# Unread matmuls in four layer norms, and three MLP units side by side behind two of them

## What is computed

```python
def _layer_norm(x, g, b):
    xf = x.astype(jnp.float32)
    mu = jnp.mean(xf, -1, keepdims=True)
    var = jnp.mean(jnp.square(xf - mu), -1, keepdims=True)
    return ((xf - mu) * lax.rsqrt(var + LN_EPS) * g + b).astype(x.dtype)

def _sq_relu_mlp(x, w1, w2):
    return jnp.square(jax.nn.relu(x @ w1)) @ w2

    for layer in range(DEPTH):
        ...
        x = _layer_norm(DEEPNORM_ALPHA * x + h, ln1_g[layer], ln1_b[layer])
        x = _layer_norm(DEEPNORM_ALPHA * x + _sq_relu_mlp(x, mlp_w1[layer], mlp_w2[layer]),
                        ln2_g[layer], ln2_b[layer])
```

## Time and profile before

| | us |
|---|---|
| median of 3 runs | 3241.9 (3241.63 to 3243.15) |
| profiled execution | 3248.51 |
| its span | 3246.7 |
| TensorE busy | 3161.2 (97%) |
| VectorE busy | 1778.5 (55%) |
| ScalarE busy | 1182.9 (36%) |
| GpSimd busy | 190.0 (6%) |
| mean granted TensorE clock, share of full | 0.982 |

### The profile page before, as it was taken

How to read it: one execution, slowest core, us unless ns; L and a number is a source line. 1 busy time by engine, 2 the same in 40 slices (tenths; PEclk the granted TensorE clock), 3 DMA queues, 4 the chain that set the end, 5 groups by cost and what they waited for, 6 DMA issues and landing times.

```text
span 3246.7 us, 42028 instructions
## 1 busy us (share of the span) xinstructions
PE 3161.2 (97%) x17280; PEld 2505.5 (77%) x17280; DVE 1778.5 (55%) x2750; ACT 1182.9 (36%) x1849; POOL 190.0 (6%) x149
## 2 busy tenths in 40 slices
PE   9999899999999889999899999999999999999999
PEld 6788778888777678887677687788877758778887
DVE  3753463343777754344577545654647754566463
ACT  4543243232444434232353423432335342343232
POOL 1221020001000020000100000000010000010000
PEclk9999899999999989999899999999999999999999
DMA  4210022222222112222212122223232212222322
GB/s 170 78 51 20 2 80 102 91 91 92 73 72 72 65 52 89 93 91 91 100 65 78 52 94 93 97 77 111 81 114 77 67 51 91 91 91 86 102 94 75
DMA packets 41563, 264.88 MB, mean 82 GB/s; under 512 B 4600, under 2 KB 4984, under 8 KB 13980
## 3 DMA queue, kind: packets, MB, share of 16 engines
q1 hardware_dynamic: 41364, 262.18, 23.7%
q10 hardware_dynamic: 8, 0.01, 0.0%
HBM read 260.07 MB, written 3.42 MB: 81 GB/s over the span
## 4 chain that ended last, share of the span: by engine, by line
PE 79%; DVE 6%; ACT 3%; issue 1%; DVEq 0%; ACTq 0%; POOL 0%; POOLq 0%
PE psum L340 23%; PE psum L342 23%; PE psum L341 23%; PE psum L1029 2%; ACT tiles L1067 1%; DVE tiles L1091 1%; PE psum L2017 1%; PE psum L2016 1%; PE psum L2018 1%; DVE w_lo L321 1%; PE psum L1928 1%; PE psum L1936 1%; PE psum L1038 1%; PE psum L690 1%; PE psum L1020 1%
## 5 line engine op out<-in xcount | busy, mean ns | idle before, releaser
L340 PE MATMUL psum<-hi,w_hi 128*128 128x512 f32 x3608 | 1447.0, 401 | 18.2 <-DVE w_lo L321 9.1
L341 PE MATMUL psum<-lo,w_hi 128*128 128x512 f32 x3608 | 1427.3, 396 | 0.0
L342 PE MATMUL psum<-hi,w_lo 128*128 128x512 f32 x3608 | 1427.2, 396 | 0.0
L313 ACT ACTIVATE w_hi<-ring 128x1024 fp32r<-128x1024 f32 (+1 forms) x495 | 505.1, 1021 | 889.0 <-PE psum L342 825.6
L340 PEld LDWEIGHTS psum<-hi,w_hi 128*128 128x128 f32 x3608 | 678.5, 188 | 189.2 <-DVE lo L590 10.2
L321 DVE TENSOR_TENSOR w_lo<-ring,w_hi 128x1024 fp32r<-128x1024 f32 (+1 forms) x495 | 592.9, 1199 | 421.4 <-ACT w_hi L313 421.3
L341 PEld LDWEIGHTS psum<-lo,w_hi 128*128 128x128 f32 x3608 | 678.5, 188 | 168.5 <-issue 7.0
L342 PEld LDWEIGHTS psum<-hi,w_lo 128*128 128x128 f32 x3608 | 677.7, 188 | 165.9
L772 DVE SCALAR_TENSOR_TENSOR xT<-xT,psum 128x512 f32<-128x512 f32 x96 | 65.9, 687 | 224.8 <-PE psum L342 224.8
L1067 ACT ACTIVATE tiles<-tiles,small 128x256 f32<-128x256 f32 (+3 forms) x176 | 95.0, 541 | 159.6 <-DVE small L1091 159.1
L1676 DVE TENSOR_TENSOR tiles<-tiles 128x512 f32<-128x512 f32 x64 | 44.3, 692 | 173.4 <-ACT tiles L1668 173.4
(11 more groups left out here) (262 smaller groups left out, 2749.6 us busy)
## 6 DMA issues: line engine op xcount, KB each, us to landing
ring<-in_weights SPq DMA_DIRECT2D x211, 1024.0 KB, 4.8
ring<-in_weights SPq DMA_DIRECT2D x28, 704.0 KB, 4.0
ring<-in_weights SPq DMA_DIRECT2D x4, 896.0 KB, 4.5
ring<-in_weights SPq DMA_DIRECT2D x3, 832.0 KB, 4.3
xT<-in_x SPq DMA_DIRECT2D x8, 256.0 KB, 5.4
tiles<-bias_repeated SPq DMA_DIRECT2D x8, 256.0 KB, 7.1
out<-xT SPq DMA_DIRECT2D x8, 256.0 KB, 2.8
held<-in_const SPq DMA_DIRECT2D x1, 1344.0 KB, 7.6
```

The source lines that it names most:

```text
L313: act.activation(self.w_hi[:, n % AHEAD, 0:UNITS[n] * P], self.raw(n), ACT.Copy).then_inc(self.hi_ready, 1)
L340: pe.matmul(out, hi, rhs.hi(first + at), start=(at == 0), stop=False)
L341: pe.matmul(out, hi, rhs.lo(first + at), start=False, stop=False)
L342: last = pe.matmul(out, lo, rhs.hi(first + at), start=False, stop=(at == end))
```

## The change

It has two parts.

First, matmuls whose result nobody reads. `idle` issues `count` matmuls in plain f32 into a bank: the 128x128 identity as weights, the 512 columns of `mask` (an attention mask in SBUF, mostly zeros) streamed past them. In `Moments.sums` one stands behind the first group of sums and one behind the last; in `layer_norm` three stand behind the second spread. All go to bank 4. So that bank 4 is free, the wait for the sixth residual tile (`added`, 6) moves up in front of the first of them. That makes five at each of the four norms, twenty in all.

Second, `three_products` takes the place of `two_products` in `squared_relu` (behind the first and the third norm). Two units run along with the arriving tiles as before, and a third follows `LAG` = 3 tiles behind. `two_products` stays behind the second and the fourth norm.

```diff
+LAG = 3
...
+    def idle(self, pe, count, bank):
+        for n in range(count):
+            pe.matmul(self.bank(bank), self.c("ident"), self.mask[:, :], start=True, stop=True)
+
+    def three_products(self, pe, outs, n, rhs, rhs_ready):
+        pe.wait_ge(self.lo_ready, n + 2)
+        for i in range(DT + LAG):
+            if i < DT:
+                pe.wait_ge(rhs_ready, i + 1)
+            if i == LAG:
+                pe.wait_ge(self.lo_ready, n + 3)
+            for u, at, out in ((n, i, outs[0]), (n + 1, i, outs[1]), (n + 2, i - LAG, outs[2])):
+                if 0 <= at < DT:
+                    w = slice(at * P, (at + 1) * P)
+                    hi, lo = self.w_hi[:, u % AHEAD, w], self.w_lo[:, u % AHEAD, w]
+                    pe.matmul(out, hi, rhs.hi(at), start=(at == 0), stop=False)
+                    pe.matmul(out, hi, rhs.lo(at), start=False, stop=False)
+                    last = pe.matmul(out, lo, rhs.hi(at), start=False, stop=(at == DT - 1))
+                    if at == DT - 1:
+                        last.then_inc(self.unit_used, 1)
...
         token_sums(pe, sq_out, self.acc, column, last=False)
+        pe.wait_ge(self.added, 6)
+        self.k.idle(pe, 1, 4)
         pe.wait_ge(self.diff_summed, DT - 2 - SHIFT)
-        pe.wait_ge(self.added, 6)
         token_sums(pe, diff_out, self.diff, column, last=False)
         pe.wait_ge(self.shifted, DT)
         token_sums(pe, diff_out, self.k.x(DT - 1), column, first=False).then_inc(self.diff_done, 1)
         pe.wait_ge(self.squared, DT)
         token_sums(pe, sq_out, self.sq[(DT - 1) % 2], column, first=False).then_inc(self.sq_done, 1)
+        self.k.idle(pe, 1, 4)
...
             spread_tokens(k, pe, k.bank(7), rstd, 1).then_inc(spread_done, 1)
+            k.idle(pe, 3, 4)
...
-            k.two_products(pe, [k.bank(0), k.bank(1)], first, rhs, rhs_ready)
-        elif t == 1 and rhs_ready is not None:
+            k.three_products(pe, [k.bank(0), k.bank(1), k.bank(2)], first, rhs, rhs_ready)
+        elif t in (1, 2) and rhs_ready is not None:
             return
```

## The result

| | before | after |
|---|---|---|
| median of 18 runs, us | 3242.7 (3240.9 to 3248.6) | 3250.2 (3243.5 to 3254.3) |
| ratio, 95% interval | 1 | 1.0018 (1.0012 to 1.0025) |
| span of the profiled execution, us | 3246.7 | 3248.5 |
| its mean granted TensorE clock | 0.982 | 0.987 |

The changed kernel is slower by 0.18%, 5.8 us by the ratio (3.9 to 8.1), 7.5 by the medians. The measured time lies in the predicted range. The forecast was +6.1 us (3248.0). All of these lie at the edge of what counts as no change (6.5 us). The profiled execution of the change took 3250.3 us, which is at the median of its runs; that of the kernel before took 3248.5, among the longest of its runs.

The account below looks back on a forecast made before the run. TensorE, busy 97% of the span near full clock, was taken as the bound. Clock falls at about three of four norms, 2.0 us each, gave +6.1 us over the median 3241.9: 3248.0 us, range 3240.5 to 3255.

Parts of the forecast that it names:

- Prices: TensorE at the norms: one unread matmul 0.86 us, a group of sums 0.89 us at full clock; 1.72 and 1.67 at half.
- Parts one and two: Unread matmuls among and behind the sums, before the first spread: each delays VectorE's centring 0.86 us, 1.72 per norm at equal clock.
- Part three: Three unread matmuls behind the last spread: full clock for first products gains at most 1.04, 1.4, 0.7 us; fourth norm none.
- Part four: Three units side by side behind the first and third norm: 0.1 us gained at each over two units, 0.2 in all.
- How often the clock falls, and what a fall costs: At the norms: the clock falls at about three of four, some later than now, so 2.0 instead of 2.35 us each.
- the +0.3 that was worked out for a full clock: Second norm, clock staying full: centring 1.7 us later, products gain 1.4, net +0.3 us.
- A: Rival: the clock holds at all four norms, delay and gain cancel, 0 us, 3241.9 us; chance 0.20.
- B: Rival: unread matmuls don't count as work for the clock, three behind the spread run at half; +16 us, 3258; chance 0.07.
- C: Rival: holes in the sums hide the first two unread matmuls and the clock holds; -6.5 to -7 us, 3235; chance 0.05.
- D: Rival: side-by-side units starve the next split, 1 to 2 us at first and third norm; inside the range, no separate chance.

Follow-up runs that it names:

- sums_alone: Kernel before plus only the two unread matmuls among and behind the sums at each norm, two units side by side: 1.0021 against the kernel before, +6.8 us.
- doubled_sums: The change with two unread matmuls instead of one in each place among and behind the sums: 1.0030 against the kernel before, +9.7 us.
- tail_alone: Kernel before plus only the three unread matmuls behind the second spread, two units side by side: 0.9991 against the kernel before, -2.9 us.
- three_alone: The change without any unread matmul, three units side by side behind the first and third norm: 0.9997 against the kernel before.
- unread_alone: The change with two units side by side as before, all five unread matmuls per norm kept: 1.0021 against the kernel before, +6.8 us.
- second_alone: Kernel before plus only the one unread matmul behind the sums at each norm: 1.0006 against the kernel before, +1.9 us.
- tail_three: The change without the two unread matmuls among and behind the sums; three behind the spread and three units stay: 0.9989 against the kernel before, -3.6 us.
- five_behind: The change with all five unread matmuls of each norm behind the second spread, three units side by side: 0.9988 against the kernel before, -3.9 us.
- first_alone: Kernel before plus only the one unread matmul among the sums at each norm: 1.0003 against the kernel before, +1.0 us.
- first_tail: The change without the unread matmul behind the sums; one among them, three behind the spread, three units: 0.9994 against the kernel before, -1.9 us.

## Why the prediction was right, and where its steps were off

**Prices.** The unread matmul was put at 0.86 us from rows of the same shape; in the changed profile one group of sums and one of them take 1.75 us (435.25 to 437.00), which is 0.89 + 0.86, and the six records behind the spread last 2.74 us, five steps of 0.43 and one record of 0.59. Right.

**Parts one and two, the chain.** +1.72 us per norm at equal clock. Measured at the second norm 6.38 against 4.66 us: right to 0.01. That a delay of the norms is passed on is seen in the profiles of sums_alone and doubled_sums, 4.5 and 9.3 us when the second block's row is reached. That all of it is passed on is not shown: at the fourth norm of the change 1.1 of the 1.7 us are.

**Part three, the clock's gain.** Forecast at most 1.0, 1.4 and 0.7 us at the first three norms; the 48 products took 1.0, 1.4 and 0.7 us less in tail_alone. In all -2.9 us by the ratio (0 to -5.8), against the 1.04 + 1.4 + 0.7 = 3.1 of the bounds. Right.

**Part four.** +-0.2 us, measured -1.0 (-3.6 to +1.9): not told from nothing, as said.

**How often the clock falls, and what a fall costs.** I took three of four norms, at 2.0 us each. In the profile it falls at three of four, later than before at the first and third norm (4.2 us after the dense work) and, at the fourth, only at 1586.4, behind the norm's spreads. Centring was 1.7, 1.7, 1.4 and 1.7 us late, where I had allowed 3.4 and 2.7 to 3.5 for a fall at the old moment. The number of falls was right; the price of one was not. Between the same VectorE instructions in both profiles (430.2 to 500.7, 803.5 to 860.1, 1190.1 to 1260.1 and 1561.8 to 1612.1 us before), the change takes 0.6, 0.3, 0.6 and 1.1 us longer: 2.6 us for the four norms, where 6.1 were forecast. The second norm is the +0.3 that was worked out for a full clock; the first and third cost 0.6 each with a fall, not 2.0. The step that was off is therefore this term, three falls at 2.0 us. One profile cannot give its mean (over the same four stretches three_alone, whose norms are those of before, is 2.1 us shorter than before), but the ratio of the runs (+5.8) does not confirm 2.0 either, because more than the norms goes into it, as the part on the spans shows. That the total came out near +6.1 is in part luck.

**Rivals.** A (the clock holds, 0 us): the number is excluded by the interval, and the clock fell at three norms of the profile. But the 2.6 us of its four norms lie between A's 0 and the forecast. B (unread matmuls don't count for the clock): excluded by the second norm, which held full clock for 11.3 us of sums, spreads and unread matmuls, and by the first products at full clock. C (holes hide them): excluded by the queue without holes and by sums_alone. D: no idle time of TensorE ahead of the next unit.

The Trainium skill, page "TensorE: Matmul & The Clock Gate", section "Part 4: PE-mode transpose", says that a matmul in transpose mode does not count as busy for the clock in the same way. Nothing here contradicts it; but a plain matmul with the identity as weights and a mostly zero stream does count: the second norm held the full clock for 11.3 us over the sums, the spreads and all five of them.

**The spans of the two profiles, and a term that the sum lacks.** The prediction gave 3252.8 us for the span of the changed kernel, if profiled: 6.1 more than before. It was 3248.5, 1.8 more. All of the 1.8 is there when the second block's row is reached (2.6 lost at the norms, 1.2 won back between 1100 and 1190 us, where the clock was low for 20.5 us instead of 23.9, and some 0.4 elsewhere); behind that both executions take the same time. So where is the rest of the +5.8 of the runs? The row consists mostly of matmuls on half the array (L1928, L1936). Where it begins and the first product behind it, in the profile of before:

```profile
2608.28 1.12 PE L1928 MATMUL psum<-tiles 64*128 64x512 f32 x2
...
2642.31 0.50 PE L340 MATMUL psum<-hi,w_hi 128*128 128x512 f32 x1
```

The same two in the changed kernel, then in second_alone:

```profile
2610.11 1.12 PE L1957 MATMUL psum<-tiles 64*128 64x512 f32 x2
...
2644.14 0.50 PE L341 MATMUL psum<-hi,w_hi 128*128 128x512 f32 x1
```

```profile
2608.28 1.12 PE L1955 MATMUL psum<-tiles 64*128 64x512 f32 x2
...
2637.52 0.50 PE L341 MATMUL psum<-hi,w_hi 128*128 128x512 f32 x1
```

34.0 us, 34.0 us and 29.2 us for the same work. The difference is the clock. Before, then second_alone (columns as in the earlier trace rows):

```profile
2615.60:2625.00 9.40, 9.40 (x14) 0.50 0.00 0
```

```profile
2615.60:2625.00 9.40, 9.40 (x27) 1.00 0.01 2
```

In the profiles of before, of the change and of unread_alone the clock stays at 1.2 GHz for 13.6 us in this row, and falls once more between 2826 and 2829 us; in ten others it stays there for 3.4 us and has no such second fall; in tail_alone it does not fall in the row at all, but at 2818. Against the short form the long one costs 4.8 us in the row and 1.5 us behind it, 6.3 together, as much as the change is worth.

The profile of before had the long form. Without it, it would have taken some 3248.5 - 6.3 = 3242.2 us (an estimate), and that is where most runs of this kernel lie: 98 of 111 took 3240.2 to 3244.6 us, 13 took 3247.2 to 3249.1, and none lies between. The profile of the change had the long form too, and took 3250.3 us, at the median of its runs. In unread_alone no run of eleven took less than 3247.6 us, and its profile, with the long form, had lost 0.3 us when it reached the row. So a part of what the change costs, perhaps the larger, is that more of its executions have the long form. How many do is not known, since each kernel has one profile. Nor is it shown why: in the three profiles with the long form the clock fell 3.4 to 3.6 us after VectorE's first instruction of the row, in the ten with the short one 2.6 to 3.4 us after it. A delay ahead of the row may move that moment, but before (3.39) and second_alone (3.40) reached the row in the same microsecond and went different ways.

Spans of single profiles are of no use for a difference of this size; the distances inside a norm are.

## What to carry to other kernels

Work inserted only to keep TensorE's clock up belongs where TensorE waits for another engine and no other engine waits for TensorE: here behind the last spread, in the 3.3 us before the first `lo` tile, where it gains 3 to 4 us (0.9989 in tail_three, 0.9988 in five_behind, the best versions tried), not in front of a result that VectorE is waiting for, where the same instruction delays that result by 0.86 us each time at full clock. A queue in which TensorE is busy without holes is not a free place even if its own work is light: look at who waits for its end. To judge it, measure from the last dense product to the first dependent instruction, norm by norm, and let the runs, not the span of one profile, give the sum. Then follow the same instructions of both profiles to the end of the program, and ask whether something else goes into the sum: here a stretch a thousand microseconds behind the last norm is worth 6.3 us by its clock alone, and it was in the profile of before, as the 6.6 us between that execution and the median, ahead of the prediction.

## What the runs showed of the hardware

- A queue of one-column matmuls without a hole does not keep the clock up: it fell 2.3 to 5.2 us after the dense work at the four norms of the kernel before, and 2.2 to 8.8 us after it in tail_three and three_alone, whose sums are the same. With one plain f32 matmul of 128x512 (0.86 us) among the sums it fell after 5.0 to 6.0 us in first_alone and after 3.7 to 6.0 us in first_tail; with one more behind them, in the changed kernel, after 4.2 us or later.
- At the first norm of the changed kernel the clock was low for 3.4 us (439.5 to 442.9), while TensorE did an unread matmul and the spreads without a hole. In the kernel before it was low for 13.6 us (437.5 to 451.2), over the sums, the spreads, a hole of 3.35 us and 4.9 us of dense products.
- TensorE can be busy all the time (9.40 of 9.40 us) and stay at 1.2 GHz: so it did from 2615.6 to 2625.0, with matmuls that use half the array (64*128, 128*64) up to 2623.4 and full ones after that. The same row ran at 2.4 GHz in another execution. Why one execution comes up and the other does not stays open.
